# Norm seams, modulation schedule and warm-up matmuls in a two-block fp32 transformer step

## The reference, cut to what matters

```
# first block
a = rms_norm(x) ; proj = a @ w_in            # q, k, v (8 heads) and u (conv branch)
mixed = concat(attention(q, k, v), conformer_conv(u)) @ w_out
h = x + rms_norm(mixed) * g
h = h + rms_norm(square(relu(rms_norm(h) @ w_ff1)) @ w_ff2) * g      # d_ff = 8192
# second block, layer "ev" (attention with a context), then layer "od" (pooling)
shift, scale, gate = split(silu(c) @ mod_w + mod_b)      # one 2048 x 6144 matrix per layer
y = attention_or_pool((rms_norm(h) * (1 + scale) + shift) @ w_in) * silu(z)
h = h + gate * rms_norm(y @ w_out)
```

## Time and profile before

| | us |
|---|---|
| median of 3 runs | 1888.36 (1885.23 to 1890.24) |
| the profiled execution's own time | 1888.55 |
| its span, first to last instruction | 1886.9 |
| PE busy | 1820.1 (96%) |
| DVE busy | 1457.7 (77%) |
| ACT busy | 900.3 (48%) |
| POOL busy | 116.1 (6%) |
| DMA | 426.94 MB, mean 226 GB/s |

### The profile page before, as it was taken

The page is one execution under the profiler, slowest core; times in us unless marked ns, Lnnn a source line. Parts: engine busy times, 40 slices in busy tenths (PEclk is TensorE's granted clock), DMA queues, the critical chain, the costliest instruction groups (busy, mean ns, idle before and its releaser), DMA issues.

```text
span 1886.9 us, 26488 instructions
## 1 busy us (share of the span) xinstructions
PE 1820.1 (96%) x10068; PEld 1573.7 (83%) x10068; DVE 1457.7 (77%) x1671; ACT 900.3 (48%) x1158; POOL 116.1 (6%) x217
## 2 busy tenths in 40 slices
PE   6999999999999999999999979999999998999997
PEld 6999978788888888888888768888888887888986
DVE  4799996778878898898788987745677677887854
ACT  5343456464434543443344447523556545445452
POOL 0100000100110000000000000000111000000000
PEclk9999999999999999999999989999999999999999
DMA  7865545948998788777977747645544684768662
GB/s 263 291 195 183 159 155 194 331 156 278 325 318 279 240 287 281 234 243 260 266 244 250 262 157 266 200 158 177 168 145 158 242 291 140 252 223 260 209 223 89
DMA packets 189737, 426.94 MB, mean 226 GB/s; under 512 B 12352, under 2 KB 12736, under 8 KB 187840
## 3 DMA queue, kind: packets, MB, share of 16 engines
q1 hardware_dynamic: 161984, 324.80, 50.7%
q0 software_dynamic: 27648, 100.68, 16.3%
HBM read 421.23 MB, written 4.21 MB: 225 GB/s over the span
## 4 chain that ended last, share of the span: by engine, by line
PE 81%; DVE 11%; DMA 4%; ACT 2%; issue 2%; SPq 0%; DVEq 0%; POOLq 0%; ACTq 0%; POOL 0%
PE banks L1831 18%; PE banks L1854 12%; PE banks L1855 12%; PE banks L1856 12%; PE banks L1833 9%; PE banks L1819 4%; PE banks L1820 4%; PE banks L1821 4%; DVE w_lo L1053 3%; DMA mod_raw<-in_ev_mod_w 2%; DVE mod_sum L1242 2%; PE banks L1894 2%; DVE mod_sum L1092 2%; PE banks L2120 1%; PE banks L2136 1%
## 5 line engine op out<-in xcount | busy, mean ns | idle before, releaser
L530 ACT ACTIVATE w_hi<-raw 128x1024 fp32r<-128x1024 f32 x552 | 579.2, 1058 | 697.9 <-PE banks L1856 330.9
L1053 DVE TENSOR_TENSOR w_lo<-raw,w_hi 128x1024 fp32r<-128x1024 f32 x552 | 666.8, 1221 | 233.5 <-ACT w_hi L530 231.4
L1831 PE MATMUL banks<-a_pair,w_hi 128*128 128x512 f32 x1536 | 546.1, 400 | 1.8 <-DVE w_lo L1053 1.5
L1833 PE MATMUL banks<-a_pair,w_lo 128*128 128x256 f32 x1536 | 431.9, 281 | 0.0
L1831 PEld LDWEIGHTS banks<-a_pair,w_hi 128*128 128x128 f32 x1536 | 289.3, 188 | 74.3 <-DVE w_lo L1053 2.2
L1092 DVE SCALAR_TENSOR_TENSOR mod_sum<-mod_raw,silu_c,mod_sum 128x1024 f32<-128x1024 f32 x240 | 301.5, 1280 | 48.0 <-DMA mod_raw<-in_ev_mod_w 24.0
L1854 PE MATMUL banks<-w_hi,b_hi 128*128 128x512 f32 x832 | 326.2, 392 | 4.2 <-DVE w_lo L1053 4.2
L1856 PE MATMUL banks<-w_hi,b_lo 128*128 128x512 f32 x832 | 323.9, 389 | 0.0
L1855 PE MATMUL banks<-w_lo,b_hi 128*128 128x512 f32 x832 | 323.7, 389 | 0.0
L1833 PEld LDWEIGHTS banks<-a_pair,w_lo 128*128 128x128 f32 x1536 | 290.9, 189 | 0.1
L1819 PE MATMUL banks<-a_pair,w_hi 128*128 128x256 f32 x768 | 222.1, 289 | 3.3 <-DVE w_lo L1053 2.9
(11 more groups left out here) (202 smaller groups left out, 1612.3 us busy)
## 6 DMA issues: line engine op xcount, KB each, us to landing
raw<-in_w_ff SPq DMA_DIRECT2D x128, 1024.0 KB, 6.7
mod_raw<-in_ev_mod_w POOLq DMA_DIRECT2D x96, 512.0 KB, 5.2
mod_raw<-in_od_mod_w POOLq DMA_DIRECT2D x96, 512.0 KB, 5.4
raw<-in_w_in SPq DMA_DIRECT2D x40, 1024.0 KB, 5.1
raw<-in_ev_w_in SPq DMA_DIRECT2D x40, 1024.0 KB, 5.8
raw<-in_od_w_in SPq DMA_DIRECT2D x32, 1024.0 KB, 6.7
...
```

The lines of the kernel that those rows point to most:

```text
L530: nc.scalar.activation(w_hi[:, s % SLOTS], raw[:, s // 2, KPS * (s % 2):KPS * (s % 2) + KPS, :], ACT.Copy).then_inc(hi_ready, 1)
L1053: nc.vector.tensor_tensor(w_lo[:, s % SLOTS], raw[:, s // 2, KPS * (s % 2):KPS * (s % 2) + KPS, :], w_hi[:, s % SLOTS].bitcast(F32), ALU.s ...
L1831: nc.tensor.matmul(out[:, f, :], wh, rows[:, :, k, :], start=s == 0 and t == 0, stop=False, skip_group_check=True)
L1833: last = nc.tensor.matmul(out[:, f, T:2 * T], wl, rows[:, 0, k, :], start=False, stop=s == STEPS - 1 and t == KPS - 1, skip_group_check=True)
```

## The change

- **Start.** The identity goes first, x is loaded in four pieces, `cols` next, then the first weight block; the small constants follow it. ACT and DVE share the squares. Each norm pair is followed by its weight split. POOL's first modulation load waits for four splits of the first block.
- **Modulation order.** The od shift moves from the ff stage to evq, evkv; the od scale from evq, evkv and the heads to the heads and evo; the od gate starts later and is denser in odg. In ff the two ev units spread wider and the scale is folded and copied out within the last blocks.
- **Seams.** The last two K steps before norms 1, 2, 4 and the end are done for the first 128 tokens, then for the other 128 (`last_steps`), and the squares, gains and products follow token tile by token tile; post_scale starts on the squares of both tiles before the second gain.
- **End.** Five residual pieces stay on DVE, three go to ACT (scale) and POOL (add); eight stores of 256 KB, five on SP's queue and three on ACT's.
- **Warm-up.** PE multiplies `ones` with `ones` (128x128x128, fp32) 16, 12, 20 and 22 times ahead of the transposes of norms 0, 1, 2 and 4.

```diff
-MOD_UNITS = [("ev_gate", 1), ("od_shift", 1), ("ev_shift", 2), ("ev_scale", 2), ("od_scale", 1), ("od_gate", 1)]
+MOD_UNITS = [("ev_gate", 1), ("ev_shift", 2), ("ev_scale", 2), ("od_shift", 1), ("od_scale", 1), ("od_gate", 1)]
+WARM = {0: 16, 1: 12, 2: 20, 4: 22}
+HEAD_HALVES = ((0,), (1, 2), (3,), (4, 5))
+DVE_PIECES = [(0, 0), (1, 0), (0, 1), (1, 1), (0, 2)]
+POOL_PIECES = [(1, 2), (0, 3), (1, 3)]
...
-    for tt in range(TT):
-        sp.dma_start(X[:, tt, :], io["x"][tt * P:(tt + 1) * P, :]).then_inc(x_first[tt], 16)
-    sp.dma_start(ident[:], io["ident"]).then_inc(const_in, 16)
-    sp.dma_start(cols[:], io["cols"]).then_inc(const_in, 16)
-    sp.dma_start(quad[:], io["quad"]).then_inc(const_in, 16)
-    sp.dma_start(qk_gain[:, 0, :], io["q_norm"].partition_broadcast(P)).then_inc(const_in, 16)
-    sp.dma_start(qk_gain[:, 1, :], io["k_norm"].partition_broadcast(P)).then_inc(const_in, 16)
-    sp.dma_start(table[:, 0:512], io["dist_neg"]).then_inc(table_in, 16)
+    sp.dma_start(ident[:], io["ident"]).then_inc(ident_in, 16)
+    for n in range(2 * TT):
+        half = slice(D // 2 * (n % 2), D // 2 * (n % 2 + 1))
+        sp.dma_start(X[:, n // 2, half], io["x"][n // 2 * P:(n // 2 + 1) * P, half]).then_inc(x_first[n], 16)
+    sp.dma_start(cols[:], io["cols"]).then_inc(cols_in, 16)
...
+        if n == 0:
+            sp.dma_start(quad[:], io["quad"]).then_inc(const_in, 16)
+            sp.dma_start(qk_gain[:, 0, :], io["q_norm"].partition_broadcast(P)).then_inc(const_in, 16)
+            sp.dma_start(qk_gain[:, 1, :], io["k_norm"].partition_broadcast(P)).then_inc(const_in, 16)
+            sp.dma_start(table[:, 0:512], io["dist_neg"]).then_inc(table_in, 16)
...
+    pool.wait_ge(split_done, 8 + 4)
     first_loads("ev_gate", "ev", 2)
     load_mod("ev_gate", "ev", 2, 1, KT)
-    first_loads("od_shift", "od", 0)
-    load_mod("od_shift", "od", 0, 1, KT)
     first_loads("ev_shift", "ev", 0)
     load_mod("ev_shift", "ev", 0, 1, KT)
     first_loads("ev_scale", "ev", 1)
     load_mod("ev_scale", "ev", 1, 1, KT)
-    first_loads("od_scale", "od", 1, "ev_scale")
-    load_mod("od_scale", "od", 1, 1, KT // 2 - 1)
+    first_loads("od_shift", "od", 0, "ev_scale")
+    load_mod("od_shift", "od", 0, 1, 12)
...
+    load_mod("od_shift", "od", 0, 12, KT)
+    first_loads("od_scale", "od", 1, "od_shift")
...
+    for n, (tt, c) in enumerate(POOL_PIECES):
+        part = slice(BW * c, BW * (c + 1))
+        pool.wait_ge(tail_scaled, n + 1)
+        nc.gpsimd.tensor_tensor(X[:, tt, part], Y[:, tt, part], X[:, tt, part], ALU.add).then_inc(tail_ready, 1)
...
+    for n in range(2 * TT):
+        tt, part = n // 2, slice(D // 2, D // 2 + BW) if n % 2 else slice(0, D // 2)
+        act.wait_ge(x_first[n], 16)
+        nc.scalar.activation(Y[:, tt, part], X[:, tt, part], ACT.Square,
+                             accum_out=ssq_part[:, tt, n % 2:n % 2 + 1]).then_inc(ssq_ready, 1)
     root(0)
-    split_hi(0, (0, 1))
-    act.wait_ge(const_in, 80)
+    act.wait_ge(cols_in, 16)
     gain = col("g_mix_pre", 0, KT)
...
+    for j in range(KT // 2):
+        norm_scaled(0, gain, a_hi, [j])
+        split_hi(0, [j])
...
+    post_scale(1, lambda: gained(6, 3, out_acc[3], None, [1]))
     dve.wait_ge(x_in, 16)
     dve.wait_ge(acc_free, 2 + ACC["ff"])
-    post_scale(1)
...
-                turn("ev_gate", 1, 0, ff_temp, p, 17)
-            elif 22 <= p < 70:
-                halves("od_shift", *spread(p, 22, 70, 32))
-            elif 70 <= p < 75:
-                turn("od_shift", 0, 0, ff_temp, p, 70)
-            elif 75 <= p < 155:
-                halves("ev_shift", *spread(p, 75, 155, 32, 3, 4))
-            elif 155 <= p < 165:
-                turn("ev_shift", 0, 1, ff_temp, p, 155)
-            elif 165 <= p < 244:
-                halves("ev_scale", *spread(p, 165, 244, 32, 3, 4))
-            elif 244 <= p < 254:
-                turn("ev_scale", 0, 2, raw_temp, p, 244)
-            if p == 132:
-                mod_out(0, [(OD_SHIFT, col("od_mod_b", 0, KT)), (EV_GATE, col("ev_mod_b", 32, KT))])
+                turn("ev_gate", 0, 0, ff_temp, p, 17)
+            elif 22 <= p < 120:
+                halves("ev_shift", *spread(p, 22, 120, 32, 3, 4))
+            elif 120 <= p < 130:
+                turn("ev_shift", 0, 1, ff_temp, p, 120)
+            elif 130 <= p < 228:
+                halves("ev_scale", *spread(p, 130, 228, 32, 3, 4))
+            elif 228 <= p < 238:
+                turn("ev_scale", 0, 2, raw_temp, p, 228)
+            if p == 68:
+                mod_out(0, [(EV_GATE, col("ev_mod_b", 32, KT))])
...
+            if p == 250:
+                mod_out(2, [(EV_SCALE, col("ev_mod_b", KT, KT)), (EV_SCALE_C, col("ev_mod_b", KT, KT))])
+                for d in (EV_SCALE, EV_SCALE_C):
+                    nc.vector.scalar_tensor_tensor(mod_cols[:, d, :], mod_cols[:, d, :], 1.0, col("ev_pre_g", 0, KT),
+                                                   ALU.add, ALU.mult)
...
-                halves("od_scale", i, 1)
+                halves("od_shift", i, 1)
         split_lo(b + 2, [3])
     dve.wait_ge(acc_free, 2 + ACC["evq"] + 4)
     rope(q_sb[1].rearrange("p (t h d) -> p t h d", t=TT, h=FT), FT)
-    run_ahead(BLOCK["evkv"], each("od_scale", 4, (1, 2, 1, 2)))
+    run_ahead(BLOCK["evkv"], each("od_shift", 4, (3, 4, 4, 3)))
     dve.wait_ge(acc_free, 2 + ACC["evkv"] + 2)
     head_norm(2, q_sb[0].rearrange("p (h d) -> p h d", h=8), 1)
     rope(q_sb[0][:, 0:512].rearrange("p (t h d) -> p t h d", t=TT, h=2), 2)
-    run_ahead(BLOCK["evkv"] + 1, each("od_scale", 10, (1, 2, 1, 2)))
+    def last_keys_beside(m):
+        each("od_shift", 18, (4, 4, 4, 2))(m)
+        if m == 3:
+            mod_turn("od_shift", 0, 0, 3, raw_temp)
+    run_ahead(BLOCK["evkv"] + 1, last_keys_beside)
...
-            mod_step("od_scale", KT // 2 + 2 * i + j // 2, j % 2)
+            for c in HEAD_HALVES[j]:
+                mod_step("od_scale", 3 * i + c // 2, c % 2)
...
-        gate = each("od_gate", 4 * (n - 1), (1, 1, 0) if n == 3 else (1, 1, 1, 1)) if n else None
         def go(m):
-            if n == 0 and m == 2:
-                mod_turn("od_scale", 0, 0, 3, raw_temp)
-            if n == 2 and m == 2:
-                mod_out(3, [(OD_SCALE, col("od_mod_b", KT, KT))])
+            if n < 2:
+                halves("od_scale", 24 + 4 * n + m, 1)
+            elif n == 2:
+                turn_parts("od_scale", 0, 1, 3, raw_temp, m, 1)
+            elif m == 0:
+                mod_out(3, [(OD_SHIFT, col("od_mod_b", 0, KT)), (OD_SCALE, col("od_mod_b", KT, KT))])
                 nc.vector.scalar_tensor_tensor(mod_cols[:, OD_SCALE, :], mod_cols[:, OD_SCALE, :], 1.0,
                                                col("od_pre_g", 0, KT), ALU.add, ALU.mult)
+            else:
+                halves("od_gate", m - 1, 1)
...
+    last_tile(0)
+    dve.wait_ge(y_squared, 2 * TT * NBLK)
+    post_scale(6, lambda: last_tile(1))
+    dve.sem_inc(acc_free, 1)
...
-    gate_steps = [(1, 1, 1, 0)] * 2 + [(1, 0, 1, 0)] * 2 + [(0, 0, 0, 0)] + [(1, 1, 1, 1)] * 2 + [(2, 2, 0, 0)]
+    gate_steps = [(1, 1, 1, 1), (1, 1, 1, 0), (1, 1, 1, 0), (1, 0, 1, 0), (0, 0, 0, 0), (2, 2, 2, 1), (2, 2, 2, 1), (2, 2, 0, 0)]
...
+    def last_steps(steps, a2, hi, lo):
+        for tt in range(TT):
+            for s, slot in steps:
+                for t in range(KPS):
+                    k = KPS * s + t
+                    o = a2[:, BW * tt:BW * (tt + 1)]
+                    ah = hi[:, k, P * tt:P * (tt + 1)]
+                    nc.tensor.matmul(o, ah, w_hi[:, slot, t, :], start=False, stop=False, skip_group_check=True)
+                    nc.tensor.matmul(o, ah, w_lo[:, slot, t, :], start=False, stop=False, skip_group_check=True)
+                    e = nc.tensor.matmul(o, lo[:, k, P * tt:P * (tt + 1)], w_hi[:, slot, t, :], skip_group_check=True,
+                                         start=False, stop=s == STEPS - 1 and t == KPS - 1)
+                if tt == TT - 1:
+                    e.then_inc(step_done, 1)
+            if tt < TT - 1:
+                e.then_inc(tile_done, 1)
...
+    def keep_warm(count):
+        for _ in range(count):
+            nc.tensor.matmul(aux[:, 2, 0:P], ones[:], ones[:], start=True, stop=True)
     def norm_product(m, b, a, form, lead):
+        keep_warm(WARM[m])
...
+    pe.wait_ge(ident_in, 16)
     pe.wait_ge(ones_ready, 1)
+    pe.wait_ge(x_first[1], 16)
...
+    first_hidden(1, "ev_gate", 1, 0)
+    ff_hidden(1, 1)
+    ff_outer(1, 4)
+    ff_hidden(2, 0)
+    ff_outer(2, 8)
+    first_hidden(3, "ev_shift", 2, 1)
+    ff_hidden(3, 1)
+    ff_outer(3, 12, True)
+    pe.wait_ge(mod_cols_ready, 3)
...
-        product(BLOCK["evo"] + n, ACC["evo"] + n, acc[(n + 1) % 2], step_tokens, b_hi, b_lo, z_ready, FT, 0)
-        if n == 1:
-            sum_mod("od_scale", 1, 3)
+        product(BLOCK["evo"] + n, ACC["evo"] + n, acc[(n + 1) % 2], step_tokens, b_hi, b_lo, z_ready, FT, 0,
+                by_tile=n == 3)
```

(8 more changed lines are left out.)

248 lines of the change are left out of this document (139 added, 109 removed).

## The result

The changed kernel takes 1916.62 us (median of 4 runs, 1915.91 to 1920.22) against 1887.09 for the kernel before beside it: ratio 1.0159, interval 1.0139 to 1.0179, 29.5 us slower. The forecast was 1906, with a range of 1879 to 1919.

What follows compares the result with a forecast made beforehand. PE was taken as the bound, busy 1820.1 of 1886.9 us. From 1888.55, gains of 17.6 off and losses of 35.4 added gave 1906 us; 1879 to 1919 was to hold 8 in 10.

Steps and rivals of the forecast that it cites:

- The sign and the cause: Whole kernel: slower, chance 0.71, mainly because moved modulation halves have a rate of their own that evkv cannot cover.
- evkv: Second block's key/value stage: 28 od_shift halves and their fold cost a 23.7 us stall plus 2 us of cold clock.
- The stall: First head of the second attention: PE waits behind DVE's od_shift fold, 23.7 us, partly already inside evkv and evz.
- the rate of a half: Modulation loads in two buffers: a pair of halves takes 7.08 us, 3.54 us a half.
- GpSimd's staging of the second head's q: At that attention's start: it waits behind the same od_shift fold and hides in it, no extra cost.
- B: Rival: every load lands in 4.2 us, a pair takes 6.2, evkv costs 12 less, total 1892; chance 0.08.
- C: Rival: loads land sooner than any row shows, evkv costs 6, odg nothing, total 1885; chance 0.05.
- evo: Behind the third evo block: PE waits 3.7 us for the last od_scale part, plus 1.2 for the clock; 4.9 us.
- odu and odg: 1.3 us for one more back-to-back half in odu, about 3.5 in odg after 6 of cover; 4.8 (1 to 11).
- The end: After PE's last matmul: pieces shared by DVE, ACT and GpSimd shorten 12.0 us to 9.3; gain 2.7 (1.5 to 4).
- The start: Before the first product: transposes begin at 10.3, first product at 16.8 instead of 21.76; gain 5.0 (3 to 7).
- The seams: Gains of 2.5 us at norm 1, 2.5 at ff's end, 3.0 at norm 2, 1.9 at norm 4.

Runs made afterwards that it cites:

- x_sched: The changed kernel with the modulation sums in the order of the kernel before, ff's sums 5% denser: 1876.03 us, ratio 0.9934 to the kernel before.
- x_light: The changed kernel with od_shift loads cut to a quarter of their columns, all columns still folded (sums wrong, for timing only): 1897.97 us.
- x_short: The changed kernel folding only a quarter of each od_shift half, loads left whole (sums wrong, for timing only): 1907.87 us.
- x_evo: The changed kernel with od_scale's four turning steps one place earlier beside evo 2: 1912.21 us.
- x_warm0: The changed kernel without any warm-up products: 1921.25 us.
- x_tail: The changed kernel with all eight end pieces on DVE, stored by SP and ACT in turn, none on GpSimd: 1913.07 us.

## Why the prediction was right, and where it was not

The sign and the cause were right, and 1916.6 lies in the range, 10.6 us above the forecast. Step by step:

- **evkv, 25.7 us forecast (23.7 and 2 for the clock), 27.7 measured.** The stall, its cause (the fold ahead of the first head's maximum) and the rate of a half were right: DVE was to be free of the sums at 1339.4 on the time scale of before; it was at 1324.0, which is 1342.8 on that scale, since evkv began 18.8 us earlier. x_sched shows that the order causes it, x_light and x_short that landing and fold share it about two to one. One step was not as forecast: GpSimd's staging of the second head's q was to hide in the fold, and it was the wait that PE's row names. It cost at most 0.9 us of its own: the probabilities were ready at 1329.0, and their transposes began at 1329.9. The Trainium skill (DMA: Bandwidth & Descriptors, Anatomy of one DMA) reckons 2.0 us and the bytes over 436 GB/s for a load, by which I estimate 3.2 us for 512 KB. The landings measured here (median 4.8, least 4.0) are above it, and the measurement decides; rivals B and C, which needed landings of 4.2 us or less throughout, are out. The same estimate for 128 KB is 2.3, which is the least that x_light shows, with a median of 2.7.
- **evo, 4.9 forecast, 5.3 measured,** the wait 3.58 (3.7) and the clock behind it; x_evo took it away whole.
- **odu and odg, 4.8 forecast (bounds 1 to 11), 13.0 measured.** This is the term that failed: the rate of a half was right here too (3.6 us), the cover was not. In odu I had 1.3 for one more back-to-back half; two halves that waited for a load stood ahead of two splits, PE waited 2.88 us, the clock fell behind it, and the curve rose by 2.9. In odg I had counted cover for the whole stage at once, 6 us of it, and a lag of 2.6 per block; the curve rose by 3.7 and 4.6 over odg 1 and 2. The rows show that each group of two halves ahead of a pair of splits can make PE wait by itself (1.5, 0.8, 0.7 and 2.1 us between 1755 and 1784), that slack gained between groups isn't kept, that the gate's sum behind the closing fold costs another 3.4, where the kernel before had 1.0, and that the clock falls once more behind it. PE in odu, then DVE and PE in odg and at its end:

```profile
1628.49 0.50 PE L1898 MATMUL banks<-a_pair,w_hi 128*128 128x512 f32 x1 [2.88 <-DVE w_lo L1089]
...
1754.37 1.29 DVE L1128 SCALAR_TENSOR_TENSOR mod_sum<-mod_raw,silu_c,mod_sum 128x1024 f32<-128x1024 f32 x1 [0.86 <-DMA mod_raw<-in_od_mod_w]
1755.58 2.35 DVE L1089 TENSOR_TENSOR w_lo<-raw,w_hi 128x1024 fp32r<-128x1024 f32 x2
1756.85 0.50 PE L1898 MATMUL banks<-a_pair,w_hi 128*128 128x512 f32 x1 [1.52 <-DVE w_lo L1089]
...
1793.08 0.40 PE L1886 MATMUL banks<-b_hi,w_hi 128*128 128x256 f32 x1 [3.40 <-DVE scratch L1816]
```

x_sched's flat -14.8 shows all of it to be the order's. (The same stretch costs 11.0, 10.5 and 13.2 us in the profiled executions of x_evo, x_warm0 and x_tail.)
- **The end, a gain of 2.7 forecast, a loss of 2.6 measured.** The stores did land 0.7 us sooner. But GpSimd's additions took 1.71 us each, above my 1.24, slowed the DVE pieces beside them from 0.67 to about 1.7, and GpSimd's drain behind them held the end for 3.4 us more; I had no term for either. In x_tail's trace the end is 4.2 us shorter.
- **The start, 5.0 forecast.** The first product came 4.7 us sooner, but by another way: the transposes began at 12.69, not at 10.3, and they and their pair work took 4.3 us, not 6.4, since the warm-ups had brought the clock up. That these two errors cancel is luck. Without warm-ups (x_warm0) the transposes began at 12.00 and the first product at 17.36, 0.3 us later than with them; nothing of that is left in u, where x_warm0 is at -3.6 and the changed kernel at -3.4. 1.3 us of the gain went back in u, as idle time for low splits (1.70 and 2.42 us ending at 74.4 and 82.8, where the kernel before waited once, 2.69), which I hadn't counted.
- **The seams, 2.5 at norm 1, 2.5 + 3.0 at ff's end and norm 2, 1.9 at norm 4 forecast; 4.4, 4.4 + 6.0 and 2.6 measured** (norm 1 counted to ff 4). The seams' lengths were right: 3.3, 6.6 and 6.0 us where I had 3.5, 7.4 and 6.0. The price of a warm-up was wrong: 0.13 us instead of 0.224, because I read a group's count of 8 as eight products when each fp32 product is two instructions. By that I left 4.9 us idle at norm 2 and gave the clock up; 2.14 were left, and it held in this execution, as it did in only three of eight. ff's end, and what its lighter load of sums did in ff 2 to 4, were under-counted.

In the profiled spans the change is +27.3 us where +17.8 was forecast. The 9.5 between them are 10.6 more of losses (8.2 in odu and odg, 2.0 in evkv, 0.4 in evo) and 5.3 at the end, less 6.4 more of gains in front of the losses. The errors partly cancel: the cause was right, the closeness of the total is in part luck.
